# Two-block transformer, one core: handovers between stages split into token halves, norm step, mixer memory and opening rearranged

## The reference

```python
def rms_norm(x, g):
    y = x * lax.rsqrt(jnp.mean(x * x, axis=-1, keepdims=True) + EPS)
    return y * g

def modulate(x, m, i):                      # m: 9 vectors of 1024 per token set, from c or c_ctx
    return x * (1 + m[:, 3 * i + 1][:, None]) + m[:, 3 * i][:, None]

def ffn_sublayer(x, m, i, g, w_in, w_out):
    u = modulate(rms_norm(x, g), m, i)
    a, b = jnp.split(u @ w_in, 2, axis=-1)   # w_in: 1024 x 5632, w_out: 2816 x 1024
    return x + 0.5 * m[:, 3 * i + 2][:, None] * ((silu(a) * b) @ w_out)

for l in range(2):
    x_lat, x_ctx = ffn_sublayer(x_lat, m_lat, 0, ...), ffn_sublayer(x_ctx, m_ctx, 0, ...)
    u_lat, u_ctx = modulate(rms_norm(x_lat, g1), m_lat, 1), modulate(rms_norm(x_ctx, g1), m_ctx, 1)
    # q, k, v, Fourier part and gates from u @ w_in; differential attention; merge; @ w_o
    x_lat = x_lat + m_lat[:, 5][:, None] * mix_l     # and x_ctx in layer 0
    x_lat, x_ctx = ffn_sublayer(x_lat, m_lat, 2, ...), ffn_sublayer(x_ctx, m_ctx, 2, ...)
```

## Time and profile before

| | us |
|---|---|
| median of 3 runs (2774.08 to 2790.99) | 2778.22 |
| the profiled execution | 2777.34 |
| its span, first to last instruction | 2775.2 |
| TensorE busy / VectorE busy / ScalarE busy | 2637.7 / 1582.6 / 997.5 |
| mean granted clock of TensorE | 0.973 |

### The profile page before, as it was taken

One profiled execution on the slowest core, in us unless ns is written; L12 is line 12 of the kernel. 1 busy time (PEld: TensorE's weight loads), 2 busy tenths in 40 slices (PEclk: granted clock), 3 DMA queues, 4 the chain that ended last, 5 costly groups with the idle time before them and its releaser, 6 DMA issues.

```text
span 2775.2 us, 35565 instructions
## 1 busy us (share of the span) xinstructions
PE 2637.7 (95%) x14510; PEld 2138.0 (77%) x14510; DVE 1582.6 (57%) x2833; ACT 997.5 (36%) x1760; POOL 52.6 (2%) x55
## 2 busy tenths in 40 slices
PE   8999989999999999999999989999999889997896
PEld 6888878867887888878888878798997777784342
DVE  4877755376446867548777364765555764444111
ACT  5222233266334322243222253755444533322111
POOL 0000000000000000000000000000000000000320
PEclk8999999999999999999999999999999899998998
DMA  7536442200322445334476323043525022157997
GB/s 309 200 143 241 157 168 91 100 22 31 122 91 85 194 172 224 129 122 167 174 288 265 121 105 122 31 183 132 210 100 202 31 92 92 62 207 307 403 373 312
DMA packets 56818, 456.44 MB, mean 164 GB/s; under 512 B 10705, under 2 KB 21329, under 8 KB 21841
## 3 DMA queue, kind: packets, MB, share of 16 engines
q1 hardware_dynamic: 49456, 446.01, 41.7%
q0 software_dynamic: 6912, 6.32, 0.7%
q10 hardware_dynamic: 288, 1.84, 0.2%
HBM read 497.11 MB, written 1.05 MB: 180 GB/s over the span
## 4 chain that ended last, share of the span: by engine, by line
PE 83%; DVE 6%; DMA 5%; ACT 3%; issue 1%; SPq 0%; POOL 0%; DVEq 0%; ACTq 0%; POOLq 0%
PE ps L513 64%; PE ps L2301 3%; PE ps L1690 3%; PE ps L3281 1%; DVE st L1511 1%; PE ps L2908 1%; PE ps L2360 1%; DMA BIG<-eup 1%; DMA wr<-ws 1%; DMA U<-edn 1%; PE ps L1223 1%; DMA U<-eup,extra_ids 1%; DMA wr<-edn 1%; DVE BIG L1523 1%; PE nb L3307 1%
## 5 line engine op out<-in xcount | busy, mean ns | idle before, releaser
L513 PE MATMUL ps<-UL,fh 128*128 128x512 f32 (+1 forms) x1408 | 513.7, 365 | 11.1 <-DVE UL L843 8.4
L513 PE MATMUL ps<-UH,fl 128*128 128x512 f32 (+1 forms) x1408 | 512.1, 364 | 0.0
L513 PE MATMUL ps<-UH,fh 128*128 128x512 f32 (+1 forms) x1408 | 511.9, 364 | 0.0
L507 DVE TENSOR_TENSOR fl<-wr,fh 128x1024 fp32r<-128x1024 f32 (+1 forms) x304 | 328.7, 1082 | 247.1 <-ACT fh L500 247.0
L500 ACT CAST fh<-wr 128x1024 fp32r<-128x1024 f32 (+1 forms) x304 | 282.7, 934 | 201.4 <-PE ps L513 181.9
L561 DVE SCALAR_TENSOR_TENSOR acc<-wr,CA 128x1024 f32<-128x1024 f32 x256 | 312.9, 1222 | 3.7
L513 PEld LDWEIGHTS ps<-UL,fh 128*128 128x128 f32 x1408 | 267.2, 190 | 55.4 <-DVE UL L843 11.4
L513 PEld LDWEIGHTS ps<-UH,fh 128*128 128x128 f32 x1408 | 267.2, 190 | 41.4
L513 PEld LDWEIGHTS ps<-UH,fl 128*128 128x128 f32 x1408 | 267.3, 190 | 41.1
L507 DVE TENSOR_TENSOR ml<-wr,mh 128x1024 fp32r<-128x1024 f32 (+1 forms) x132 | 153.8, 1168 | 220.6 <-ACT mh L500 220.3
L513 PE MATMUL ps<-HH,fh 128*128 128x512 f32 (+1 forms) x704 | 255.2, 363 | 0.0
(11 more groups left out here) (553 smaller groups left out, 4221.0 us busy)
## 6 DMA issues: line engine op xcount, KB each, us to landing
wr<-ws SPq DMA_DIRECT2D x135, 2048.0 KB, 7.9
wr<-ws SPq DMA_DIRECT2D x32, 1408.0 KB, 6.0
wr<-eup SPq DMA_DIRECT2D x32, 1024.0 KB, 12.9
BIG<-eup SPq DMA_DIRECT2D x22, 1024.0 KB, 17.4
wr<-edn SPq DMA_DIRECT2D x16, 1024.0 KB, 17.2
wr<-ws SPq DMA_DIRECT2D x11, 1024.0 KB, 7.0
BIG<-edn SPq DMA_DIRECT2D x11, 1024.0 KB, 18.5
X<-eup SPq DMA_DIRECT2D x6, 1024.0 KB
```

What stands on the lines that cost most here:

```text
L507: e.tensor_tensor(lv, raw_tile(sp.units[n]), hv.bitcast(F32), ALU.subtract).then_inc(*low_done.inc("low", event))
L513: i = e.matmul(out, l, r, start=first and n == 0, stop=last and n == len(pairs) - 1, skip_group_check=True)
```

## The change

At the four handovers with 512 tokens (first feed-forward to mixer in both layers, mixer 0 to feed-forward, feed-forward to feed-forward):

- The last output tiles (6 and 7 of a feed-forward, 5 to 7 of the mixer; `HELD`) are computed for the latents first and then for the context; the latent means (`pe_means_first`, in `NB`) are put into the context part. The context means (`pe_means_second`) get a PSUM bank of their own, in the middle of the next stage's first products.
- The next stage's first four units (three before in a mixer) run over the latents, then over the context (`pe_first_halves`), not staggered as before. `act_turn` and `dve_turn` give the orders of the two other engines, with four weight tiles between the norm tiles.
- The norm tile is made per half in three steps: VectorE multiplies by gain and inverse root at once, ScalarE adds the shift and rounds to the high part, VectorE adds the shift again and subtracts the high part, in place. All inverse roots come from Ln and Exp; `act_root`, `dve_root` and `pe_spread` go from these places. The last feed-forward (256 tokens) gets the same norm steps with the order of `act_norm` and `dve_norm`, two weight tiles ahead of the Ln.
- The mixer's inputs take the place of the feed-forward's `UH` and `UL`, its split weights use the buffers `FS`, and q, k, v, the attention buffers and the merged tile are moved; the first units of a stage can be split as each of the last units of the stage before is used up.
- The opening loads the first feed-forward weights third (`wmodk` 0, 2, `fin`, `wmodk` 1, `fin`, `wmodk` 3). TensorE starts the first two units on channels 0 to 511, with the rows of the later two modulation chunks between them.

The core of the diff:

```diff
...
-SETS = {"ffn": 4, "in": 3, "gate": 3}
+FFN_SETS = {(0, 0): (3, 0, 1, 2), (0, 1): (3, 2, 0, 1), (1, 0): (3, 2, 0, 1), (1, 1): (3, 1, 2, 0)}
+MIX_SETS = {0: (0, 1, 2), 1: (2, 0, 1)}
+HELD = {"ffn": (6, 7), "mix": (5, 6, 7)}
...
-    out = [("wmodk", ch) for ch in FIRST_CHUNKS]
+    out = [("wmodk", ch) for ch in FIRST_CHUNKS[0:2]]
...
+                if (l, f, half, p) == (0, 0, 0, 0):
+                    out.insert(len(out) - 1, ("wmodk", FIRST_CHUNKS[2]))
+                    out.append(("wmodk", FIRST_CHUNKS[3]))
...
-        MUH, MUL = over("MUH", 4096 + 20480, [128, 8, 512]), over("MUL", 0, [128, 8, 512])
-        MGH, MGL = over("MGH", 4096 + 4096, [128, 8, 512]), over("MGL", 4096 + 10240, [128, 8, 512])
-        MS = [(over(f"mh{i}", 4096 + 14336 + 2048 * i, [128, 1024]), over(f"ml{i}", 4096 + 15360 + 2048 * i, [128, 1024]))
-              for i in range(3)]
+        MGH, MGLA, MGLB = over("MGH", 16384, [128, 8, 512]), over("MGLA", 20480, [128, 6, 512]), over("MGLB", 27648, [128, 2, 512])
+        MGL = [MGLA[:, j, :] for j in range(6)] + [MGLB[:, j, :] for j in range(2)]
...
             pe_mod_cols(e, 2)
-            pe_mod_rows(e, 1)
-            pe_mod_cols(e, 1)
-            pe_mod_rows(e, 3)
-            pe_mod_cols(e, 3)
...
+            for _ in range(2):
+                high_parts(e, sp, sp.next_one())
             e.wait_ge(*at("gains", 0))
             for k in range(4):
                 norm(k)
-            for _ in range(4):
+            for _ in range(2):
                 high_parts(e, sp, sp.next_one())
             e.wait_ge(*at("gains", 1))
             for k in range(4, 8):
             dve_gains(e, segs, gain, scale, slice(0, 4))
             dve.mark("gains", 0)
             scaled(3)
+            for k in range(2):
+                low_parts(e, sp, sp.next_one())
+                low(k)
+            low(2)
+            low(3)
             dve_mod_rows(e, 1)
-            low(0)
+            for k in (4, 5):
+                low_parts(e, sp, sp.next_one())
+                scaled(k)
+            dve_mod_rows(e, 3)
+            scaled(6)
+            scaled(7)
             dve_mod_cols(e, 1)
-            low(1)
-            low(2)
-            dve_mod_rows(e, 3)
-            scaled(4)
-            low(3)
-            scaled(5)
             dve_mod_cols(e, 3)
             dve_gains(e, segs, gain, scale, slice(4, 8))
             dve.mark("gains", 1)
-            for k in (6, 7, 8, 9):
-                low_parts(e, sp, sp.next_one())
-                if k < 8:
-                    scaled(k)
             for k in range(4, 8):
                 low(k)
...
+        def pe_means_first(e, prev, nb_free):
+            e.wait_ge(*at("scaled", nb_free, 7))
+            e.wait_ge(*at("square sum", prev, 6, 0))
+            e.matmul(NB[:, 0:256], ones, RS[:, 0:256], start=True, stop=False, skip_group_check=True)
+            e.wait_ge(*at("square", prev, 7, 0))
+            e.matmul(NB[:, 0:256], ones, rot.of("stats", prev)[:, 0:256], start=False, stop=True, skip_group_check=True).then_inc(
+                *sums.inc("stats", prev, 0))
+        def pe_means_second(e, prev, held, name):
+            b, old = psum.take("scaled", name, 7)
+            if old:
+                e.wait_ge(*at(*old))
+            e.wait_ge(*(at("square sum", prev, 5, 1) if 5 in held else at("square sum", prev, 5)))
+            e.matmul(b[:, 0:256], ones, RS[:, 256:512], start=True, stop=False, skip_group_check=True)
+            e.wait_ge(*at("square", prev, 6, 1))
+            e.matmul(b[:, 0:256], ones, rot.of("square sum", prev, 6)[:, 256:512], start=False, stop=False, skip_group_check=True)
+            e.wait_ge(*at("square", prev, 7, 1))
+            e.matmul(b[:, 0:256], ones, rot.of("stats", prev)[:, 256:512], start=False, stop=True,
+                     skip_group_check=True).then_inc(*sums.inc("stats", prev, 1))
+            sums.mark("square sum", prev, 6)
+            sums.mark("stats", prev)
...
+        def act_roots(e, name, prev, c):
+            b = norm_bank(name, c)
+            e.wait_ge(*at("stats", prev, c))
+            e.activation(b, b, ACT.Ln, scale=1.0 / D, bias=eps[:, :]).then_inc(*act.inc())
+            e.wait_ge(*act.now())
+            e.activation(b, b, ACT.Exp, scale=-0.5).then_inc(*act.inc("spread", name, c))
...
+        def act_u_high(e, name, c, shift, k):
+            lo, hi = BOTH[c]
+            e.wait_ge(*at("scaled", name, c, k))
+            e.activation(UH[:, k, lo:hi], unsplit(k, lo, hi), ACT.Identity, bias=shift[:, c, k:k + 1]).then_inc(
+                *act.inc("u high", name, c, k))
+        def dve_scaled(e, name, c, k):
+            lo, hi = BOTH[c]
+            if k == 0:
+                e.wait_ge(*at("spread", name, c))
+            e.scalar_tensor_tensor(out=unsplit(k, lo, hi), in0=X[:, k, lo:hi], scalar=AB[:, c, k:k + 1], in1=norm_bank(name, c),
+                                   op0=ALU.mult, op1=ALU.mult).then_inc(*dve.inc("scaled", name, c, k))
+        def dve_u_low(e, name, c, shift, k):
+            lo, hi = BOTH[c]
+            e.wait_ge(*at("u high", name, c, k))
+            e.scalar_tensor_tensor(out=UL[:, k, lo:hi], in0=unsplit(k, lo, hi), scalar=shift[:, c, k:k + 1],
+                                   in1=UH[:, k, lo:hi].bitcast(F32), op0=ALU.add, op1=ALU.subtract).then_inc(
+                                       *dve.inc("u", name, c, k))
...
+        def act_turn(e, name, prev, shift, sp):
+            held = HELD[prev[0]]
+            def tile():
+                high_parts(e, sp, sp.next_one())
+            if prev[0] == "mix":
+                tile()
+            act_roots(e, name, prev, 0)
+            if prev[0] == "mix":
+                act_square_half(e, prev, 5, 1)
+            else:
+                tile()
+            act_u_high(e, name, 0, shift, 0)
+            tile()
+            act_u_high(e, name, 0, shift, 1)
+            act_u_high(e, name, 0, shift, 2)
+            act_square_half(e, prev, 6, 1)
+            act_u_high(e, name, 0, shift, 3)
+            act_u_high(e, name, 0, shift, 4)
+            tile()
+            act_square_half(e, prev, 7, 1)
+            for k in range(5, 8):
+                act_u_high(e, name, 0, shift, k)
+            tile()
+            act_roots(e, name, prev, 1)
             for k in range(8):
-                tiles(early[2 + k])
-                low(k)
+                act_u_high(e, name, 1, shift, k)
+        def dve_turn(e, name, prev, segs, gain, scale, shift, sp, add):
+            held = HELD[prev[0]]
+            def tile():
+                low_parts(e, sp, sp.next_one())
+            dve_gains(e, segs, gain, scale)
+            for j in held:
+                add(j, 0)
+                if j < 7:
+                    dve_square_sum_half(e, prev, held, j, 0)
+            e.wait_ge(*dve.now())
+            if prev[0] == "mix":
+                tile()
+                add(5, 1)
+                dve_square_sum_half(e, prev, held, 5, 1)
+            for k in range(3):
+                dve_scaled(e, name, 0, k)
+            if prev[0] != "mix":
+                tile()
+            dve_u_low(e, name, 0, shift, 0)
+            dve_u_low(e, name, 0, shift, 1)
+            dve_scaled(e, name, 0, 3)
+            dve_u_low(e, name, 0, shift, 2)
+            add(6, 1)
+            tile()
+            dve_scaled(e, name, 0, 4)
+            dve_u_low(e, name, 0, shift, 3)
+            add(7, 1)
+            for k in range(5, 8):
+                dve_scaled(e, name, 0, k)
+                dve_u_low(e, name, 0, shift, k - 1)
+            dve_u_low(e, name, 0, shift, 7)
+            tile()
+            tile()
+            dve_scaled(e, name, 1, 0)
+            for k in range(8):
+                if k < 7:
+                    dve_scaled(e, name, 1, k + 1)
+                    if k == 6:
+                        dve.mark("scaled", name, 7)
+                dve_u_low(e, name, 1, shift, k)
+        def act_norm(e, name, prev, shift, sp):
+            for _ in range(2):
+                high_parts(e, sp, sp.next_one())
+            act_roots(e, name, prev, 0)
+            high_parts(e, sp, sp.next_one())
+            for k in range(8):
+                act_u_high(e, name, 0, shift, k)
+                if k == 1:
+                    high_parts(e, sp, sp.next_one())
+        def dve_norm(e, name, gain, scale, shift, sp):
+            dve_gains(e, LAT, gain, scale)
+            for _ in range(2):
+                low_parts(e, sp, sp.next_one())
+            e.wait_ge(*dve.now())
+            dve_scaled(e, name, 0, 0)
+            dve_scaled(e, name, 0, 1)
+            for k in range(8):
+                if k in (0, 2):
+                    low_parts(e, sp, sp.next_one())
+                dve_u_low(e, name, 0, shift, k)
                 if k + 2 < 8:
-                    scaled(k + 2)
+                    dve_scaled(e, name, 0, k + 2)
+            dve.mark("scaled", name, 7)
...
```

(74 more changed lines are left out.)

312 lines of the change are left out of this document (165 added, 147 removed).

## The result

| | before | changed |
|---|---|---|
| median of the runs on one chip, us | 2778.8 (2774.08 to 2790.99) | 2748.53 (2744.66 to 2750.1) |
| span of the profiled execution | 2775.2 | 2748.3 |
| mean granted clock | 0.973 | 0.977 |

The ratio of the times is 0.9879, with a 95% interval of 0.9858 to 0.9899: 28 to 39 us faster. The forecast was 2749. The same kernel, measured again beside other experiments, gave 2752.62 (ratio 0.9902, 0.9881 to 0.9922).

A forecast was written before the change was run, and what follows sets the result against it. TensorE, busy 95%, was taken as the bound, with 48.1 us missing at four handovers. Gains of 26.0 there and 4.0 at the opening, less 0.6 at the last feed-forward, made 29.4: 2749 us, own range 2745 to 2754.

The forecast's parts named there:

- The schedule of a handover: Feed-forward to mixer, timed from the last latent product's issue: first finished norm tile at 7.0 us, 0.5 us of stall left.
- Halves: Over four handovers, 1308 products of 256 columns replace 654 of 512, costing TensorE 8.7 us more.
- Means: Fp32 mean products on TensorE, five at each of four handovers at 0.44 us, cost 8.8 us.
- Stalls: TensorE waits left at the handovers: two of 0.5 us, ahead of the mixers, 1.0 us in all.
- The clock: At the handovers no gap is long enough to halve TensorE's clock, so the granted clock stays at 1.0.
- VectorE as the new bound: At each handover VectorE's queue stalls TensorE and the clock falls, 3.7 us each, 15 lost: 2764 us; chance 0.14.
- The slow form of the norm step: SCALAR_TENSOR_TENSOR with both tensors in SBUF runs at half rate, 4 us a handover, 16 in all: 2765 us; chance 0.03.
- Halves bound by their weight loads: At the handovers, 256-column products cannot overlap their 0.19 us weight loads, costing 92 us more: 2841 us; chance 0.03.
- The memory and release: Relaid mixer memory lets the next stage's first tiles be split during the output stage; alone costed at nothing.
- The opening: At the kernel's start, dense products begin at 27.4 us instead of 38.67; 4.0 us won.
- the opening gives nothing: At the kernel's start, early products run at half clock as before, so nothing is won: 2753 us; chance 0.13.
- The last feed-forward: With 256 tokens, two first weight tiles ahead of Ln and Exp delay its start: 0.6 us lost, between 0 and 2.4.

The follow-up runs named there:

- late means: Changed kernel with the latent means put one output tile later, in feed-forward and mixer: 2765.12 us, ratio 0.9945.
- 960 pairs: Changed kernel with 960 products of 512 columns in layer 0's second feed-forward turned into 1920 of 256: 2765.22 us, ratio 0.9944.
- late release: Changed kernel with the next stage's first four weight buffers all freed only by the last unit of the stage before: 2780.62 us, ratio 0.9998.
- opening alone: Kernel before the change with only the new opening put in: 2774.42 us, ratio 0.9975.
- memory alone: Kernel before the change with only the relaid mixer memory, new split-weight buffers and their early release, every order as before: 2783.8 us, ratio 1.0004.
- old opening: Changed kernel with load order, modulation chunks and first feed-forward start as in the kernel before: 2749.64 us, ratio 0.9885.

## Why the prediction held, step by step

**The schedule of a handover: right to within 1 us.** The view of waits shows none of TensorE at any of the four handovers of the changed kernel. The latent means come after 15 context products, 16 x 0.12 = 1.92 after the issue of the last latent one, so in the changed profile T0 is 393.04 - 1.92 = 391.12. TensorE, ScalarE and VectorE of the first handover:

```profile
393.04 0.59 PE L819 MATMUL nb<-RS,CC 128*128 128x256 f32 x2
393.46 0.59 PE L821 MATMUL nb<-rot,CC 128*128 128x256 f32 x2
...
402.87 0.39 PE L516 MATMUL ps<-UL,fh 128*128 128x256 f32 x1
403.10 0.28 PE L516 MATMUL ps<-UH,fl 128*128 128x256 f32 x1
```

```profile
394.58 0.37 ACT L846 ACTIVATE nb<-nb 128x256 f32<-128x256 f32 x1
395.21 1.05 ACT L503 CAST fh<-wr 128x1024 fp32r<-128x1024 f32 x1 [0.27 <-PE ps L516]
```

```profile
396.29 1.23 DVE L510 TENSOR_TENSOR fl<-wr,fh 128x1024 fp32r<-128x1024 f32 x1
397.44 1.10 DVE L867 SCALAR_TENSOR_TENSOR UL<-BIG,M,UH 128x256 fp32r<-128x256 f32 x2
...
404.93 0.48 DVE L867 SCALAR_TENSOR_TENSOR UL<-BIG,M,UH 128x256 fp32r<-128x256 f32 x1 [0.18 <-ACT UH L854]
405.33 2.35 DVE L510 TENSOR_TENSOR fl<-wr,fh 128x1024 fp32r<-128x1024 f32 x2
...
414.05 0.48 DVE L867 SCALAR_TENSOR_TENSOR UL<-BIG,M,UH 128x256 fp32r<-128x256 f32 x1 [0.18 <-ACT UH L854]
```

| us after T0 | predicted | measured |
|---|---|---|
| end of Exp | 3.9 | 3.8 |
| first weight tile, high part done | 5.05 | 5.1 |
| its low part done | 6.55 | 6.4 |
| last latent norm tile | 14.8 | 14.3 |
| fourth weight tile | 17.2 | 16.6 |
| last context norm tile | 24.4 | 23.4 |

**The terms.** Halves: 8.7, and 13.4 ns a pair in the experiment, against the 13 of the sum. Means: the chain of the changed kernel shows 0.43 for each of the five products, 2.2 a handover, 8.6 against 8.8. Broadcast rows 1.78 in the second handover's chain, so 3.6 against 3.2. Lambda product 0.12 twice against 0.4 in all. Stalls: the only one on VectorE's work in the first handover is the 0.11 at 402.87 to 403.10, where I had written 0.5; about 0.2 against 1.0. Sum 21.3 against 22.1, and 48.1 - 21.3 = 26.8 gained where the count says 26.5 and the prediction 26.0. The two misses went in opposite directions and were small: VectorE's entries came a little closer behind one another than I had taken.

**The clock.** Predicted at 1.00 in the handovers, and it is. The late means show that this was not luck of the rows but a margin of 2 us, with 6.8 us of half clock right behind it.

**The rivals at the handovers.** VectorE as the new bound (2764): not so here. The late means came to nearly the same time, 2765, by another sum: 5.7 and 5.9 us at the handovers into a mixer and 2.0 at the two others together, where the rival had 3.7 at each, so the likeness of the times is chance. The slow form of the norm step: not so.

```profile
L867 DVE SCALAR_TENSOR_TENSOR UL<-BIG,M,UH x72: 471/479/487, 397.4 to 1878.8; 128x256 fp32r<-128x256 f32 x72
```

```profile
L861 DVE SCALAR_TENSOR_TENSOR BIG<-X,AB,nb x40: 464/473/481, 395.0 to 1877.7; 128x256 f32<-128x256 f32 x40
...
L854 ACT ACTIVATE UH<-BIG,M x72: 492/508/513, 396.2 to 1878.2; 128x256 fp32r<-128x256 f32 x72
```

(Each line: shortest, median and longest in ns.) With all sources in SBUF the operation takes 0.479, with the inverse root in PSUM 0.473, as fast as the nearest rows. The bias-only rounding on ScalarE takes 0.508, between the 0.45 that I took and the bound of 0.60, and as VectorE sets the chain that cost nothing. Halves bound by their weight loads (2841): the 960 pairs refute it.

**The memory and release, costed at nothing alone.** The experiment bears that out, and the way it was put is still too weak. Its value in the chain is the whole point: at the three handovers where the change releases earlier, taking that away leaves 638 products of 731, no more than the 637 before. The sum came out right because it was made for the parts together; a sum edit by edit would have been wrong.

**The opening: 4.0 predicted, 2.9 measured.** The mechanism is the one described: products start early on half of the channels, and the rows of the later chunks stand among them. The first product was forecast at 27.4. In the profiles of the new opening it came between 27.34 (the late release) and 30.05 (the changed kernel). The late release first:

```profile
11.41 7.13 PE L621 MATMUL nb<-BIG,CC 128*128 128x512 f32 x16 [1.20 <-ACT BIG L639]
27.34 0.77 PE L516 MATMUL ps<-UL,fh 128*128 128x512 f32 x1 [3.16 <-DVE UL L685]
```

```profile
12.75 8.68 PE L621 MATMUL nb<-BIG,CC 128*128 128x512 f32 x16 [2.55 <-ACT BIG L639]
21.35 3.64 PE L588 MATMUL ps<-wr,BIG 128*32 128x512 f32 x32
...
30.05 0.77 PE L516 MATMUL ps<-UL,fh 128*128 128x512 f32 x1 [3.12 <-DVE UL L685]
```

The granted clock in the changed kernel, in windows of the same stretch:

```profile
12.50:15.90 3.40, 3.15 (x4) 0.50 0.97 414
...
29.50:33.00 3.50, 2.95 (x7) 0.51 1.03 440
33.00:43.00 10.00, 10.00 (x59) 1.00 0.99 397
```

The step of the first product was right: where the sum of the opening's squares begins at 11.41 and takes 7.13, as in the earlier trace rows, the product is at 27.34. In the changed kernel's profile the half clock falls into that sum, it begins 1.35 later and takes 8.68, and the rows that start at 21.35 and all behind them are late by that. This comes and goes with the execution: 8.68 to 8.83 in three of eight with the new opening (the changed kernel twice, the opening alone) and 8.82 in one of four with the old (the memory alone). Those three hold 1504, 1506 and 1504 products; the other five 1507 to 1513, mean 1510.0, and so 14.7 over the old mean, 3.3 us.

Two terms were off, in opposite directions. I took 4.0, between the clock full from 36.5 (3.4) and full from 33 (4.9), and in this profile it is full from 33. And a wait was not in the sum: TensorE waits for the weight tile of a later unit, 60.92 instead of 59.82, 1.1 us, which the packed start leaves behind. The view of waits shows it in all eight executions with the new opening, and not in those with the old. 4.9 - 1.1 = 3.8 is what the sum would have said with both, against the 3.3.

The rival "the opening gives nothing" is refuted by the opening alone, 4 to 10 us faster.

**The last feed-forward: 0.6 lost predicted, 0.1 to 1.0 lost** (298 and 291 products in the two profiles, 299 before). With two more executions of this order (297 with the old opening, 294 with the late means) and two more of the old one (301 and 300) the means are 295 and 300: 5 products, 0.6 us. Its step was right as well: the two tiles ahead of the Ln lengthen the gap.

**What the forecast did not have.** The attention stretch below took 2 to 3 us in this one execution and stands in no term. Whether the change has a part in it is open, as said below. The terms were right to a few us in all, and that the median came within 0.5 us of 2749 is luck: the same kernel measured again is 3.6 above it, and the two profiled executions differ by 27.2 (2777.34 and 2750.1) where the sum had 29.4.
